# Attention with rotating score banks, a ninth row a head ahead, products ahead of turns, and outputs turned and added by one product

## The reference

```python
def one_block(args):
    qi, qc = args
    sc = jnp.einsum('bhqd,bhkd->bhqk', qi, k).astype(jnp.float32) * scale
    mask = key_chunk[None, :] <= qc[:, None]
    sc = jnp.where(mask, sc, -jnp.inf)
    p = jax.nn.softmax(sc, axis=-1).astype(v.dtype)
    return jnp.einsum('bhqk,bhkd->bhqd', p, v)
```

## Time and profile before

| | us |
|---|---|
| median of three runs | 2501.58 (2498.33 to 2503.56) |
| profiled execution, its own time | 2496.99 |
| its span | 2495.2 |
| TensorE busy in it | 2236.1 (90%) |
| VectorE / ScalarE / GpSimd busy | 1077.6 / 916.3 / 406.5 |
| mean granted TensorE clock | 0.946 |

### The profile page before, as it was taken

One profiled execution on the slowest core, in us unless ns is written; L12 is line 12 of the kernel. 1 busy time (PEld: TensorE's weight loads), 2 busy tenths in 40 slices (PEclk: granted clock), 3 DMA queues, 4 the chain that ended last, 5 costly groups with the idle time before them and its releaser, 6 DMA issues. The chain is left out here.

```text
span 2495.2 us, 33539 instructions
## 1 busy us (share of the span) xinstructions
PE 2236.1 (90%) x11536; PEld 1853.5 (74%) x11536; DVE 1077.6 (43%) x1842; ACT 916.3 (37%) x1715; POOL 406.5 (16%) x254
## 2 busy tenths in 40 slices
PE   6999999999979999999678849988898875899998
PEld 5888888777868888888557737777777764677787
DVE  6000000000034554454356427767677766565663
ACT  7111111011034444444353216655655654343441
POOL 1222223214011111111022200000000003420220
PEclk9999999999989999999789859999999997899999
DMA  5222221223023333332665460223232107663751
GB/s 178 76 77 71 68 70 60 97 97 109 34 73 98 96 99 97 97 93 67 206 200 173 139 153 7 68 65 67 65 66 42 33 18 227 179 198 114 193 168 68
DMA packets 212448, 256.32 MB, mean 103 GB/s; under 512 B 38944, under 2 KB 137888, under 8 KB 208672
## 3 DMA queue, kind: packets, MB, share of 16 engines
q1 hardware_dynamic: 187616, 208.31, 29.4%
q10 hardware_dynamic: 23616, 43.00, 4.6%
q0 software_dynamic: 1152, 4.19, 0.5%
HBM read 157.41 MB, written 98.04 MB: 102 GB/s over the span
## 5 line engine op out<-in xcount | busy, mean ns | idle before, releaser
L1728 ACT ACTIVATE pT<-turn 128x512 fp32r<-128x512 f32 (+1 forms) x320 | 158.4, 533 | 203.5 <-PE turn L1855 202.9
L1785 DVE TENSOR_TENSOR pT<-turn,pT 128x512 fp32r<-128x512 f32 (+1 forms) x320 | 184.1, 606 | 92.5 <-ACT pT L1728 92.4
L66 PE MATMUL bankD<-hT_hi,shared_w_hi 128*128 128x512 f32 x512 | 212.2, 415 | 11.7 <-POOLq L676 11.7
L66 PE MATMUL bankA<-hT_hi,shared_w_hi 128*128 128x512 f32 x544 | 212.7, 391 | 0.0
L67 PE MATMUL bankA<-hT_lo,shared_w_hi 128*128 128x512 f32 x544 | 212.0, 390 | 0.0
L68 PE MATMUL bankA<-hT_hi,shared_w_lo 128*128 128x512 f32 x544 | 211.9, 390 | 0.0
L1771 DVE TENSOR_REDUCE chunk_min<-scores 128x1 f32<-128x512 f32 (+2 forms) x320 | 184.5, 606 | 61.3 <-PE scores L1841 37.3
L68 PE MATMUL bankD<-hT_hi,shared_w_lo 128*128 128x512 f32 x512 | 201.7, 394 | 0.0
L67 PE MATMUL bankD<-hT_lo,shared_w_hi 128*128 128x512 f32 x512 | 200.9, 392 | 0.0
L66 PE MATMUL scores<-k_sb,q_sb 96*128 96x512 f32 (+2 forms) x320 | 132.4, 414 | 73.3 <-ACT probs L1718 36.3
L1718 ACT ACTIVATE probs<-scores,least 128x1024 f32<-128x1024 f32 (+2 forms) x192 | 167.1, 871 | 38.5 <-DVE least L1778 37.4
(11 more groups left out here) (233 smaller groups left out, 4659.3 us busy)
## 6 DMA issues: line engine op xcount, KB each, us to landing
projT<-stage ACTq DMA_DIRECT2D x68, 256.0 KB, 2.4
shared_w_raw<-in_w_in_dram SPq DMA_DIRECT2D x32, 512.0 KB, 4.4
projT<-d_stage ACTq DMA_DIRECT2D x64, 256.0 KB, 2.4
e_l_in<-projT SPq DMA_DIRECT2D x64, 256.0 KB, 4.6
gateTok<-stage ACTq DMA_DIRECT2D x32, 256.0 KB, 2.0
shared_w_lo<-hgTok SPq DMA_DIRECT2D x16, 512.0 KB, 3.4
knT<-b_out SPq DMA_DIRECT2D x32, 256.0 KB, 2.8
vTok<-b_out SPq DMA_DIRECT2D x32, 256.0 KB, 2.9
```

Of the source, the lines that this page charges most:

```text
L66: pe.matmul(out, a_hi, b_hi, start=first, stop=False)
L1728: act.activation(pT[:, at % RING, 0, r0 * P:], turn[:, TURN_AT[tile] % 3, r0 * P:], ACT.Copy)\
L1785: dve.tensor_tensor(pT[:, at % RING, 1, r0 * P:], turn[:, TURN_AT[tile] % 3, r0 * P:], pT[:, at % RING, 0, r0 * P:].bitcast(F32), ALU.subt ...
```

## The change

It has five parts. (1) The first nine rows of the next head (`LED`), not eight, are computed in the second part of a head, and the tiles are dealt to the steps by a table, `TILES_AT`. (2) In block 2 each row starts in another bank (`3 * r`, modulo 4), and `chunks_of` cuts the pieces so that none wraps around. (3) TensorE does the values of the step before ahead of the step's turns, and in a step without tiles (rows 0 and 1) ahead of the scores too; ScalarE does `oT` first in a step. (4) `oT` is turned by a true product with `fold`, two identity matrices of 64 one above the other, which turns and adds the halves at once into 64 columns; `o_lo` and `o_sum` go, and VectorE multiplies straight from PSUM. (5) The inverse of the sums is made when the block is done.

```diff
@@ -1527,21 +1527,19 @@
 
 
 AHEAD = 2
-LED = 2 * TPB
+TURN_RING = 3
+LED = 2 * TPB + 1
 
 
 def attention_schedule():
 
-
-
-    def tiles(*blocks):
-        return [(b, j) for b in blocks for j in range(TPB * (b + 1))]
-
-    def dealt(some, n):
-        return [some[i * len(some) // n:(i + 1) * len(some) // n] for i in range(n)]
-
-    steps = [[LED + r, some, None, None] for r, some in enumerate(dealt(tiles(0, 1), TPB) + dealt(tiles(2), TPB))]
-    steps += [[r, some, None, None] for r, some in enumerate(dealt(tiles(3), LED))]
+    TILES_AT = {9: 4, 10: 3, 11: 3, 12: 4, 13: 3, 14: 3, 15: 4,
+                0: 0, 1: 0, 2: 1, 3: 2, 4: 2, 5: 2, 6: 2, 7: 3, 8: 4}
+    tiles = [(b, j) for b in range(NB) for j in range(TPB * (b + 1))]
+    steps = []
+    for row in [*range(LED, TT), *range(LED)]:
+        steps.append([row, tiles[:TILES_AT[row]], None, None])
+        tiles = tiles[TILES_AT[row]:]
     steps += [[None, [], None, None], [None, [], None, None]]
     for s in range(len(steps) - 1):
         for b, j in steps[s][1]:
@@ -1578,15 +1576,20 @@
     def s_bank(i, c):
 
         b, r = i // TPB, i % TPB
-        return c + (r if b == 0 else 2 * (r % 2) if b == 1 else 0)
+        return (c + (r if b == 0 else 2 * (r % 2) if b == 1 else 3 * r if b == 2 else 0)) % 4
+
+    def chunks_of(i, piece):
+
+        b = i // TPB
+        cut = min(1 if s_bank(i, 0) == 3 else 2, b + 1)
+        return (0, cut) if piece == 0 else (cut, b + 1)
 
     def pieces_before(i, c):
 
         need = 0
         for (t, piece), at in PIECE_AT.items():
             if t < i:
-                b = t // TPB
-                used = {s_bank(t, x) for x in range(2 * piece, min(2 * piece + 2, b + 1))}
+                used = {s_bank(t, x) for x in range(*chunks_of(t, piece))}
                 if s_bank(i, c) in used:
                     need = max(need, at + 1)
         return need or PIECE_AT[TT - 1, s_bank(i, c) // 2] + 1 - PIECES
@@ -1610,10 +1613,9 @@
         RING = 6
         pT = sb("pT", [P, RING, 2, BLK], F32R)
         oT = sb("oT", [P, BLK])
-        o_lo = sb("o_lo", [P, TPB, VD])
-        o_sum = sb("o_sum", [P, TPB, VD])
         o_out = sb("o_out", [P, 2, TPB, VD])
         ident = sb("ident_c", [P, P])
+        fold = sb("fold", [P, VD])
         early_q = sb("early_q", [P, P], F32R)
         late_k = sb("late_k", [P, P], F32R)
         mask_raw = sb("mask_raw", [P, 2, P])
@@ -1641,10 +1643,8 @@
         turn_read = sem("turn_read")
         pv_done = sem("pv_done")
         o_copied = sem("o_copied")
-        o_lo_ready = sem("o_lo_ready")
         total_ready = sem("total_ready")
         inv_ready = sem("inv_ready")
-        o_sum_ready = sem("o_sum_ready")
         o_ready = sem("o_ready")
         o_stored = [sem("o_stored0"), sem("o_stored1")]
 
@@ -1656,6 +1656,8 @@
             @block.sync
             def _(sp):
                 sp.dma_start(ident[:], ident_d).then_inc(const_in, 16)
+                for half in range(2):
+                    sp.dma_start(fold[half * VD:(half + 1) * VD, :], ident_d[0:VD, 0:VD]).then_inc(const_in, 16)
                 for u in range(2):
                     for part in range(2):
                         sp.dma_start(k_sb[PE_ROWS, u, part].bitcast(F32), kpT[part]).then_inc(kp_in, 16)
@@ -1706,10 +1708,10 @@
             def _(act):
                 def exponentials(h, i, piece):
                     b, r = i // TPB, i % TPB
-                    first, end = 2 * piece, min(2 * piece + 2, b + 1)
+                    first, end = chunks_of(i, piece)
                     n = min(end * BLK, (i + 1) * P) - first * BLK
-                    bank = s_bank(i, 0)
-                    src = scores[:].rearrange("p b n -> p (b n)")[:, (bank + first) * BLK:(bank + first) * BLK + n]
+                    bank = s_bank(i, first)
+                    src = scores[:].rearrange("p b n -> p (b n)")[:, bank * BLK:bank * BLK + n]
                     if piece == 0:
                         act.wait_ge(least_ready, h * TT + (i + 1))
                         if r == 0 and i < LED and not is_first(h):
@@ -1725,7 +1727,7 @@
                     at = TILE_AT[tile]
                     act.wait_ge(turned, h * TURNS + (TURN_AT[tile] + 1))
                     act.wait_ge(pv_done, h * TILES + (at + 2))
-                    act.activation(pT[:, at % RING, 0, r0 * P:], turn[:, TURN_AT[tile] % 3, r0 * P:], ACT.Copy)\
+                    act.activation(pT[:, at % RING, 0, r0 * P:], turn[:, TURN_AT[tile] % TURN_RING, r0 * P:], ACT.Copy)\
                        .then_inc(hi_ready, 1)
 
                 act.sem_inc(exp_done, 1)
@@ -1733,29 +1735,25 @@
 
                 def head(h, more):
                     for i, tiles, done, o_block in STEPS:
-                        for tile in tiles[:AHEAD]:
-                            hi_part(h, tile)
+                        row_of = h + 1 if i is not None and i < LED else h
                         if done is not None:
                             act.wait_ge(pv_done, h * TILES + (TILE_AT[done, TPB * (done + 1) - 1] + RING + 2))
                             if done > 0:
                                 act.wait_ge(turned, h * TURNS + (TURN_AT["o", done - 1] + 1))
                             act.activation(oT[:], o_acc[:], ACT.Copy).then_inc(o_copied, 1)
+                        for tile in tiles[:AHEAD]:
+                            hi_part(h, tile)
                         if i is not None and (more or i >= LED):
-                            exponentials(h + 1 if i < LED else h, i, 0)
+                            exponentials(row_of, i, 0)
                         for tile in tiles[AHEAD:]:
                             hi_part(h, tile)
-                        if i is not None and i >= 2 * TPB:
-                            exponentials(h, i, 1)
-                        if o_block is not None:
-                            at = TURN_AT["o", o_block]
-                            act.wait_ge(turned, h * TURNS + (at + 1))
-                            if o_block > 0:
-                                act.wait_ge(o_sum_ready, h * NB + o_block)
-                            act.activation(o_lo[:], turn[:, at % 3].rearrange("p (t n) -> p t n", n=P)[:, :, VD:], ACT.Copy)\
-                               .then_inc(o_lo_ready, 1)
+                        if i is not None and i >= 2 * TPB and (more or i >= LED):
+                            exponentials(row_of, i, 1)
 
                 for i in range(LED):
                     exponentials(0, i, 0)
+                    if i >= 2 * TPB:
+                        exponentials(0, i, 1)
                 with act.Fori(0, HEADS - 1) as h:
                     head(h, True)
                 head(HEADS - 1, False)
@@ -1782,11 +1780,10 @@
                     r0 = max(0, j - TPB * b)
                     at = TILE_AT[tile]
                     dve.wait_ge(hi_ready, h * TILES + (at + 1))
-                    dve.tensor_tensor(pT[:, at % RING, 1, r0 * P:], turn[:, TURN_AT[tile] % 3, r0 * P:],
+                    dve.tensor_tensor(pT[:, at % RING, 1, r0 * P:], turn[:, TURN_AT[tile] % TURN_RING, r0 * P:],
                                       pT[:, at % RING, 0, r0 * P:].bitcast(F32), ALU.subtract).then_inc(turn_read, 1)
 
-                def outputs(h, b):
-                    at = TURN_AT["o", b]
+                def inverse(h, b):
                     n = h * NB + (b + 1)
                     if b >= 2:
                         dve.tensor_tensor(total[:], sums[:, b, :, 0], sums[:, b, :, 1], ALU.add).then_inc(total_ready, 1)
@@ -1794,26 +1791,30 @@
                         dve.tensor_copy(total[:], sums[:, b, :, 0]).then_inc(total_ready, 1)
                     dve.wait_ge(total_ready, n)
                     dve.reciprocal(inv[:], total[:]).then_inc(inv_ready, 1)
-                    dve.wait_ge(o_lo_ready, n)
-                    dve.tensor_tensor(o_sum[:], turn[:, at % 3].rearrange("p (t n) -> p t n", n=P)[:, :, 0:VD], o_lo[:],
-                                      ALU.add).then_inc(o_sum_ready, 1)
-                    dve.wait_ge(o_sum_ready, n)
+
+                def outputs(h, b):
+                    at = TURN_AT["o", b]
+                    n = h * NB + (b + 1)
                     dve.wait_ge(inv_ready, n)
+                    dve.wait_ge(turned, h * TURNS + (at + 1))
+                    dve.wait_ge(o_stored[b % 2], h * 32 + (b // 2 * 16 + 16))
+                    dve.tensor_tensor(o_out[:, b % 2], turn[:, at % TURN_RING, 0:TPB * VD].rearrange("p (t n) -> p t n", n=VD),
+                                      inv[:].unsqueeze(2).to_broadcast([P, TPB, VD]), ALU.mult).then_inc(o_ready, 1)
+                    dve.wait_ge(o_ready, n)
                     dve.sem_inc(turn_read, 1)
-                    dve.wait_ge(o_stored[b % 2], h * 32 + (b // 2 * 16 + 16))
-                    dve.tensor_tensor(o_out[:, b % 2], o_sum[:], inv[:].unsqueeze(2).to_broadcast([P, TPB, VD]), ALU.mult)\
-                       .then_inc(o_ready, 1)
 
```

(21 more changed lines are left out.)

## The result

The changed kernel takes **2579.49 us** (median of four runs, 2574.87 to 2583.67) against 2499.95 for the kernel before beside it (2494.35 to 2503.56). The ratio is 1.0323, with a 95% interval of 1.0301 to 1.0345: some 80 us slower. The forecast was 2555 with a range of 2522 to 2586. The sign, the mechanism and the range hold; the size was too small by 24 us.

What follows compares the result with a forecast made beforehand. TensorE was taken as the bound, with idle from the chain through ScalarE and VectorE. +6.2 us a head gives 43 for seven, plus 10 for the last: +53, profiled 2550, median 2555 us; range 2522 to 2586.

Steps and rivals of the forecast that it cites:

- two chains: Attention steps: turns to next row's scores, 2.97 us; turns to a tile's values or its turn bank's reuse, 2.06 us.
- The chain: Heavy rows: turns, two hi parts, exponential, next scores take 2.97 us; 1.24 of turns beside it leaves 1.73 idle.
- Waits of a head: TensorE's waits in a full-clock head: 10.0 us in heavy rows and 4.5 in light ones, 14.5 against 9.2 before.
- 5.3 in five: Exponential's waits at heavy rows: row 10 0.15 us, row 11 1.05, row 13 1.1 and 0.4, row 14 1.73, row 15 0.83.
- A fourth turn: Four-tile steps, three turn banks: waits 1.1 us at row 9, 1.15 at row 8; at row 12 within the exponential's chain.
- The ninth row: Row 8 computed in the previous head, with rotating banks: removes the 1.62 us idle at row 9, most at row 10.
- The output product: Each block's output: four fold products take 0.90 us against 0.44 for four turns; 0.46 more, +14.7 us over 32 blocks.
- The sum for a head: Full-clock head: 68.2 less 9.2 plus 14.5 plus 1.8 gives 75.3, down to 74.0; 74.4 taken, +6.2 a head.
- The last head: No scores beside its last six tile steps; turns follow every 3.15 us instead of 1.81, some 10 us more than 61.1.
- The clock: Slow stretches of the attention stage: present loss kept, granted clock not moving from 0.93 by more than 0.04.
- The rival, to which I gave 0.15: Heads of the attention stage: longer stalls make the clock fall more, twice today's loss, some +28 us, 2583; chance 0.15.
- the loads of `fold`: Start of the attention stage: two small loads fall where TensorE waits for larger ones, costing 0.

Runs made afterwards that it cites:

- the even dealing: Changed kernel with turns ahead of values and three tiles with rows 9 to 15 and 0, two with rows 1 to 8: 2490.87 us, ratio 0.9978.
- the three tried alone: Kernel before with one part each: values ahead of turns with oT first, ratio 1.0426; output product with fold, 1.0091; rotating banks, 0.9942.
- the 175 increments: Changed kernel with 175 semaphore increments on TensorE ahead of its first scores, moving its loop along the instruction stream: 2577.57 us, ratio 1.0312.

## Why the prediction was right, and where it was too small

- *The order uncovers two chains*: right, and undoing the order takes the whole loss away (82 us). The chain was forecast at 2.97 us and measured 2.95 ahead of the scores of row 14; the idle time there, forecast at some 1.5, was 1.48.
- *Waits of a head*, forecast 14.5. The waits of the full-clock head alone are

```profile
PE turn L1856 <- DVE pT L1783: 3.3, 4, 0.9
PE scores L66 <- ACT probs L1720: 2.3, 2, 1.5
PE o_acc L1868 <- DVE pT L1783: 1.5, 3, 0.8
PE turn L1901 <- DVE pT L1783: 1.3, 2, 0.7
PE turn L1901 <- ACT oT L1743: 0.8, 1, 0.8
PE o_acc L1868 <- ACT oT L1743: 0.8, 1, 0.8
```

  These are 13 waits of together 10.0 us, or 12.6 with the 0.2 that I add to each. The size is near, the places less so. The exponential holds TensorE up for 2.3 us in two places (the second chunk of row 11, and row 14), where I had 5.3 in five; the scores of rows 13 and 15 follow almost without a stall. Fourth turns, values and output products wait for lo parts for 6.1 (7.9 with the addition; forecast 7.4), `oT` for 1.6 (2.0; forecast 1.9). A fourth turn waits in four steps of a head, not in three: that in the step of row 12 (0.47 us) was said to lie within the exponential's chain.
- *The ninth row*: no wait for banks at row 9, as forecast. What that gains is within the measurement.
- *The output product* at 0.90 us: the scores start 0.91 after it (1939.07 to 1939.98), so that was right; but four turns of `oT` took 0.36 and 0.41 (1952.21 to 1952.57, 1939.87 to 1940.28) where I had 0.44. The difference is 0.50 or a little more, at the upper bound. By the Trainium skill's rule (TensorE: Matmul & The Clock Gate, Part 1, the section on 56 ns) eight such passes would take an estimated 0.23; the trace does not agree for these products. The passes cost about what was said, but the forecast counted nothing for the clock: by themselves in the kernel before they made +24 us and not +14.7.
- *The sum for a head*: 74.4 was forecast and 76.07 measured; 1.7 a head too little, 12 us over seven, and above the 74 to 75.3 that was to be its sign. With the measured waits (12.6) the same sum gives 73.4, so some 2.7 us of the head are in no wait. They stand as busy time: start to start and without idle time, the turns of `probs` take 15.6 us of this head against 14.0 in the head of the earlier trace rows, the score and mask products 28.0 against 26.5. Why these go slower is not shown.
- *The last head*: +10 forecast, +17.4 measured. The mechanism is there (7 waits of values, 4.5 us), but 20.5 us of it ran at half clock, where the last head before had none:

```profile
2105.90:2126.40 20.50, 16.93 (x58) 12.67 (x58) 5.93 (x9) 5.21 (x9) 0.00 (x0) 0.50 0.03 6
```

- *The clock*: the forecast left the present loss as it is. For the loop that held. In the six heads from the second to the seventh, the time at 1.2 GHz is 47.8 us before and 51.2 after; beyond six times the full-clock head, and without the two branches, they lose 21.7 us before and 18.2 after. It failed in the last head, where 20.5 of the 26 us more at 1.2 GHz lie (75 to 101 in the stage). The rival, to which I gave 0.15, said 2583, and the result lies nearer to it (3.5 away) than to the forecast (24); but it said that every head would lose more, and that did not happen, so its number is near by luck. Idle time does not tell the clock either: the changed kernel with turns first (55.6 idle, 38 low) and the kernel before (58.1 and 75) wait about as long, and the even dealing has the least idle of all and more low time again. The Trainium skill (TensorE: Matmul & The Clock Gate, A second HAM failure mode) says of another kernel that micro-idles between matmul groups make the clock oscillate. Every kernel here has such idles and falls to 1.2 GHz now and again, which agrees; how long it stays there does not follow from them.
- *The loop's place and the loads of `fold`* were counted at 0. The stage starts 4.5 us later than before; other kernels here start it anywhere between 1470.8 and 1476.1 with or without `fold`, so this is not shown to come from the loads. The loop's place cost 7 us and was missed altogether.
- *Where the missing time lies*: the spans differ by 84.9 where 53 was forecast. Cut at the last output product of each head, the stage divides without overlap. Up to the end of the first head it is 97.3 us against 86.0: 5 us more than the forecast's 6.2, of which 3.4 are the scores of row 8, which now stand ahead of the loop too, at 1.2 GHz; the forecast did not count them there, nor their absence in the last head. The six heads are 484.1 against 430.9: 16 more than forecast, 9.5 of it the two branch instructions (4.84 and 4.69 longer than before) and the rest the heads' excess, less what the clock gave back. The last head is 7.4 over. The late start is 4.5, and what follows the stage gives 2.0 back. So the terms that were sized wrong are the head (1.7 too small, seven times), the last head (10 for 17.4) and the branch (0 for some 7).

## What to carry to other kernels

Put between two dependent steps of a chain the work that needs neither: here values belong behind the turns, and the new order cost 82 us though it added no work. Before letting one consumer's input go first, follow what its delay does to the other; both times that the exponential went ahead of hi parts (of all, or of the second), the kernel lost over 60 us. Try the parts of a change one by one: of the three tried alone, one was worth 14.5 us and the bundle hid it.

## What the runs showed of the hardware

*A loop's back branch can wait for its code.* Transfers in the DMA rows over two passes of the loop, of the changed kernel (1655 to 1975 us), then of the same kernel with the 175 increments (1665 to 1980):

```profile
q1 hardware_dynamic: 10816, 16.78, 23.6%
q8 instruction: 18, 0.29, 0.5%
```

```profile
q1 hardware_dynamic: 10816, 16.78, 23.9%
```

The columns are packets, MB, share of 16 engines. The data are the same, and the code loads are gone, as they are before the change. Each of the 18 packets carries 16384 bytes; in the whole run there are 53 against 35 before. So TensorE can keep a loop of 1666 to 1733 instructions, or load it anew in each pass, after how it lies in the stream. Loads in the middle of a pass cost nothing that shows: the only waits for "issue" in the loop are the two at the branch, 5.67 and 5.51 us. The clock was at its lower level around the first one:

```profile
1654.00:1660.00 6.00, 0.34 (x2) 0.15 (x1) 0.42 (x1) 0.00 (x0) 0.00 (x0) 0.50 0.45 101
1651.90:1665.60 13.70, 7.56 (x27) 6.44 (x27) 2.68 (x6) 1.30 (x3) 0.00 (x0) 0.50 0.61 123
```

It had fallen at 1651.9, before the branch. At three ends of heads without such a wait a low stretch lasts 6.8 us (from 1573.4, 1737.3 and 1976.2) and at two there is none; at the two with the wait it lasts 13.7.

The Trainium skill (Runtime: NRT & Kernel Launch, Instruction fetch mechanics) says that instructions come in blocks of 16 KiB, which are 256 of them, and that a taken branch whose target is not held forces a fetch before execution goes on. The trace agrees with the size of a block (16384 bytes) and with the wait. It says also that "there's no instruction cache that benefits from spatial locality"; the kernel before, with no code load between 1617 and 1922 us while two passes of its loop run, speaks against that.

*Less idle does not mean more clock.* The granted clock of the stage was 0.97 with 78.7 us of idle time (order and outputs undone) and 0.90 with 53.6 (`fold` alone in the kernel before). What decides it here stays open.
